# A two-layer encoder step: branch B's decay rows loaded once and kept, its running sums made earlier, and two steps of VectorE placed elsewhere

## The reference, cut to what matters

```python
for l in range(DEPTH):                                   # DEPTH = 2
    p = split_proj(rmsnorm(x, g_norm[l]) @ w_in[l])
    qa, ka, va, qi, ki, wi = a_inputs(p, pos)
    o_a = dsa_prompt(qa, qi, wi, ka, va, ki)             # attends to the top 256 keys by index score
    qb, kb, vb, lf = b_inputs(p, b_f[l])
    o_b = fox_prompt(qb, kb, vb, jnp.cumsum(lf, axis=1)) # branch B, below
    qc, kc, vc = c_inputs(p)
    o_c = band_prompt(qc, kc, vc, c_bias[l])             # own chunk and 8 before it
    mk, mv = mem_kv(mem_prompt, g_mem[l], w_mem_kv[l])
    o_m = mem_attend(m_query(p), mk, mv)                 # 256 memory tokens
    x = x + merge(p, o_a, o_b, o_c, o_m, w_out[l])

def fox_attend(q, k, v, fq, fk, qpos, kpos):
    logits = jnp.einsum('bqhd,bkhd->bhqk', q, k) * HEAD_DIM ** -0.5
    logits = logits + jnp.swapaxes(fq, 1, 2)[..., :, None] - jnp.swapaxes(fk, 1, 2)[..., None, :]
    logits = jnp.where((kpos[None, :] <= qpos[:, None])[None, None], logits, -jnp.inf)
    return jnp.einsum('bhqk,bkhd->bqhd', jax.nn.softmax(logits, axis=-1), v)
```

## Time and profile before

| | |
|---|---|
| median of 3 runs | 1775.59 us (1773.81 to 1777.07) |
| the profiled execution | 1776.22 us |
| its span in the trace | 1774.4 us |
| busy, share of the span | PE 97%, DVE 57%, ACT 39%, POOL 13% |
| mean granted clock of PE | 0.994 |
| DMA | 177.75 MB, 100 GB/s over the span |
| branch B's row loads | 24, of 256 to 1024 KB |

### The profile page before, as it was taken

The page is one execution under the profiler, slowest core; times in us unless marked ns, Lnnn a source line. Parts: engine busy times, 40 slices in busy tenths (PEclk is TensorE's granted clock), DMA queues, the critical chain, the costliest instruction groups (busy, mean ns, idle before and its releaser), DMA issues.

```text
span 1774.4 us, 25988 instructions
## 1 busy us (share of the span) xinstructions
PE 1724.7 (97%) x8678; PEld 902.0 (51%) x8678; DVE 1008.3 (57%) x2709; ACT 692.6 (39%) x1657; POOL 222.0 (13%) x398
## 2 busy tenths in 40 slices
PE   7999999999999899999999999989999999999998
PEld 3544555555555455555444345545555544555553
DVE  3646876787778633332235288767877776333322
ACT  3542333433343344453224323333334433445531
POOL 0232211100000000001012332111000000000000
PEclk9999999999999999999999999999999999999999
DMA  6433533323122222112431425433231223220121
GB/s 249 116 138 90 180 133 132 140 77 105 45 111 90 91 67 76 58 53 64 120 121 49 162 79 178 133 140 121 78 108 42 107 93 96 71 97 36 43 73 46
DMA packets 57026, 177.75 MB, mean 100 GB/s; under 512 B 10128, under 2 KB 24304, under 8 KB 53824
## 3 DMA queue, kind: packets, MB, share of 16 engines
q1 hardware_dynamic: 39424, 125.88, 20.9%
q0 software_dynamic: 17472, 50.22, 8.6%
HBM read 149.09 MB, written 30.07 MB: 101 GB/s over the span
## 4 chain that ended last, share of the span: by engine, by line
PE 87%; DVE 6%; DMA 3%; ACT 2%; issue 2%; ACTq 0%; DVEq 0%; POOL 0%; SPq 0%
PE psX L828 58%; PE psT L786 9%; PE psS L944 6%; PE psX L1011 6%; DMA bias<-scratch_fp 2%; PE psS L856 2%; DVE lower L1221 1%; DVE work L1439 1%; PE psX L986 1%; PE psS L786 1%; PE psS L917 1%; PE psX L786 1%; DVE sc L1382 1%; PE psS L910 0%; PE psS L875 0%
## 5 line engine op out<-in xcount | busy, mean ns | idle before, releaser
L828 PE MATMUL psX<-wring,hT 128*128 128x512 f32 (+1 forms) x2592 | 1170.5, 593 | 5.4 <-ACT gate L1109 3.7
L828 PEld LDWEIGHTS psX<-wring,hT 128*128 128x128 f32 x2592 | 468.8, 191 | 480.5 <-issue 478.3
L1221 DVE TENSOR_SCALAR_CACHE_REDUCE lower<-sc,thr 128x640 uint8<-128x640 f32 (+5 forms) x462 | 407.3, 934 | 19.0 <-issue 12.7
L1160 ACT ACTIVATE work<-work,stat 128x256 f32<-128x256 f32 (+7 forms) x288 | 199.9, 694 | 309.5 <-DVEq L1442 306.4
L1169 ACT COPY work<-psT 128x512 f32<-128x512 f32 (+2 forms) x352 | 157.3, 489 | 339.2 <-PE psT L786 337.3
L786 PE MATMUL psT<-con,work 128*128 128x128 f32 x1080 | 158.9, 279 | 8.8 <-ACT kv L1128 8.8
L786 PEld LDWEIGHTS psT<-con,work 128*128 128x128 f32 x1080 | 123.1, 141 | 85.0 <-issue 73.2
L1439 DVE CUSTOM_DVE_ANT_0 work<-psS,bias 128x640 f32<-128x640 f32 (+7 forms) x144 | 103.8, 721 | 102.0 <-PE psT L786 36.5
L1439 DVE CUSTOM_DVE_ANT_0 work<-psS,sc 128x384 f32<-128x384 f32 (+5 forms) x48 | 42.8, 892 | 78.5 <-PE psT L786 74.8
L1487 POOL DMA_DIRECT2D scratch_oscr<-gate x54 | 30.3, 561 | 373.7 <-DVEq L1473 353.9
L944 PE MATMUL psS<-kv,qT 64*128 64x512 f32 (+3 forms) x384 | 69.9, 482 | 0.0
(11 more groups left out here) (195 smaller groups left out, 1537.7 us busy)
## 6 DMA issues: line engine op xcount, KB each, us to landing
wring<-in_w SPq DMA_DIRECT2D x20, 2048.0 KB, 8.4
cache<-in_kB SPq DMA_DIRECT2D x16, 512.0 KB, 8.0
cache<-in_vB SPq DMA_DIRECT2D x16, 512.0 KB, 5.2
cache<-in_kC SPq DMA_DIRECT2D x16, 512.0 KB, 6.5
cache<-in_vC SPq DMA_DIRECT2D x16, 512.0 KB, 4.9
scratch_oscr<-gate POOLq DMA_DIRECT2D x54, 128.0 KB, 2.0
hT<-scratch_oscr SPq DMA_DIRECT2D x18, 384.0 KB, 3.6
bias<-scratch_fp POOLq DMA_DIRECT2D x6, 1024.0 KB, 5.3
```

Source lines behind the costliest of these rows:

```text
L828: mm = pe.matmul(X.ap(use)[:, 0:w], lhs, wv[:, kt, 0:w], start=(kt == 0), stop=(kt == KT - 1))
L1160: nc.scalar.activation(x, x, ACT.Exp, scale=-1.0, bias=stats(p)[:, 0, i:i + 1], accum_out=stats(p)[:, 1, i:i + 1]).then_inc(probs.sem, 1)
L1221: v.tensor_scalar(lower[:, at:at + STRIP_L[t]], sc[:, o], thr[:, n:n + 1], 0.0, ALU.is_lt, ALU.add, accum_out=below[:, n:n + 1])
```

## The change

1. The decay rows of all four heads are loaded once a layer, for all 1024 keys, in four DMAs (`decays("near")` for the first 256 keys, `decays("far")` for the rest), into `bias` and into `xr`, which isn't in use then. For each tile POOL's `close` copies the tile's own 128 columns of a head pair aside, drains, adds the mask in place, signals and drains; `reopen` copies the plain columns back when the logits are done, and drains. The per-pack loads are gone.
2. `wrow` stands ahead of `Q 3` and of the projection `B2 ST_`.
3. A step Z takes over the inverting and scaling on DVE, and stands ahead of T and L in `advance`, so ahead of the unit's selection.
4. `pace` spreads the selection up to unit (M1, 3).

```diff
--- before.py
+++ after.py
@@ -174,6 +174,8 @@
             if is_sample(pack) and pack[2] + 1 < PAIRS:
                 j = pack[2] + 1
                 emit("Q", (pack[0], f"s{j}", j, 1))
+        if prev:
+            emit("Z", prev)
         if prev and not fresh:
             emit("T", prev, 0)
         if pack:
@@ -282,6 +284,7 @@
         emit("Pp", "B1", ST_, 3, 6)
         emit("iw", 0)
         emit("P", "B1", ST_)
+        emit("wrow")
         emit("Q", 3)
         emit("Pp", "B2", ST_, 0, 3)
         emit("is", 2)
@@ -289,7 +292,6 @@
         emit("is", 3)
         emit("TR", "B1", ST_)
         emit("P", "B2", ST_)
-        emit("wrow")
         emit("Q", ("B", "s0", 0, 1))
 
         units = [(c, t) for pair in (("B1", "B2"), ("C1", "C2")) for t in [ST_] + TILES[:NT] for c in pair][2:]
@@ -303,7 +305,7 @@
 
                 rounds += topk_steps()
                 spare[0] = 0.0
-                pace[0] = sum(cost(x) for x in rounds) / (units.index(("A2", ST_)) - units.index(("B1", 0)) - 1)
+                pace[0] = sum(cost(x) for x in rounds) / (units.index(("M1", 3)) - units.index(("B1", 0)) - 1)
             settle()
             if t < NT and c in ("B2", "C2", "M1", "A2"):
                 queue += packs_of(c[0], t)
@@ -513,7 +515,10 @@
         bias = sb("bias", H * 5 * P + SKEYS)
         gateA = bias[:, 0:(NT + 1) * W].rearrange("p (t c) -> p t c", c=W)
         gmem = bias[:, 0:D]
-        rows_b = bias[:, 0:2 * D]
+
+
+        dec = [bias[:, 0:2 * SEQ].rearrange("p (h c) -> p h c", h=2), xr[:, :, :]]
+        plain = bias[:, 2 * SEQ:2 * SEQ + H * P].rearrange("p (g h c) -> p g h c", g=2, h=2)
         strips = bias[:, 0:H * 5 * P].rearrange("p (h c) -> p h c", h=H)
         sbias_ = bias[:, H * 5 * P:]
 
@@ -623,7 +628,7 @@
         cache_loaded = [Signal(sem(f"cache{k}_loaded"), cache_loads[k::RING], lambda u: 16 * cdmas(u)) for k in range(RING)]
 
         b_packs = [p for p in packs if p[1][0] == "B" and not is_sample(p[1])]
-        pbias = Signal(sem("prompt_bias_loaded"), b_packs, lambda e: 16)
+        pbias = {e: Signal(sem(f"decays_{e}_loaded"), each(e), lambda e: 32) for e in ("near", "far")}
         masked = Signal(sem("prompt_bias_masked"), b_packs)
         strips_loaded = Signal(sem("strips_loaded"), each("C"), lambda e: 16)
         sbias_loads = [("B", j) for j in range(PAIRS)] + [("C", 0)]
@@ -675,11 +680,6 @@
             if br == "A":
                 return hT[:, first:first + n, t * P:(t + 1) * P]
             return gate[:, t, first * P:(first + n) * P].rearrange("p (g c) -> p g c", g=n)
-
-        def decays(pack):
-
-            n, L = heads(pack), blocks(pack) * P
-            return rows_b[:, 0:n * L].rearrange("p (h c) -> p h c", h=n)
 
         def tile_of(l, n):
 
@@ -1416,7 +1416,7 @@
                             b_ = sbias_[:, 0:L]
                         elif br == "B":
                             dve.wait_ge(*masked.on(p))
-                            b_ = decays(p)[:, i, :]
+                            b_ = dec[h // 2][:, h % 2, 0:L]
                         elif br == "C":
                             if (h, t) == (0, 0):
 
@@ -1440,7 +1440,7 @@
                         if i >= heads(p) - 2:
                             last.then_inc(S.empty(u).sem, 1)
                         dve.drain().then_inc(logits.sem, 1)
-                elif k == "T" and s[2] == buffers(s[1])[-1]:
+                elif k == "Z":
 
                     p = s[1]
                     br, t, h0, nh = p
@@ -1504,19 +1504,33 @@
                         pool.dma_start(d["xr"][h * P:(h + 1) * P, :], d["xl"][h:h + 1, :].to_broadcast([P, XL])
                                        ).then_inc(lines.sem, 16)
 
-            def prompt_bias(p):
+            def decays(part):
+
+                c0, c1 = {"near": (0, 2 * P), "far": (2 * P, SEQ)}[part]
+                for g_ in range(2):
+                    src = bass.AP(d["fp"].tensor, 2 * g_ * SEQ + c0, [[0, P], [SEQ, 2], [1, c1 - c0]])
+                    pool.dma_start(dec[g_][:, :, c0:c1], src).then_inc(pbias[part].sem, 16)
+
+            def close(p):
 
                 _, t, h0, n = p
-                L = (t + 1) * P
-                src = bass.AP(d["fp"].tensor, h0 * SEQ, [[0, P], [SEQ, n], [1, L]])
-                pool.dma_start(decays(p), src).then_inc(pbias.sem, 16)
-
-            def prompt_mask(p):
-
-                own = decays(p)[:, :, blocks(p) * P - P:]
-                pool.wait_ge(*pbias.on(p))
-                g.tensor_tensor(own, own, con[:, C_TRI:C_TRI + P].unsqueeze(1).to_broadcast([P, heads(p), P]), ALU.add
-                                ).then_inc(masked.sem, 1)
+                part = "near" if t < 2 else "far"
+                pool.wait_ge(*pbias[part].on(part))
+                tri = con[:, C_TRI:C_TRI + P].unsqueeze(1).to_broadcast([P, 2, P])
+                for g_ in range(h0 // 2, (h0 + n) // 2):
+                    g.tensor_copy(plain[:, g_], dec[g_][:, :, t * P:(t + 1) * P])
+                pool.drain()
+                for g_ in range(h0 // 2, (h0 + n) // 2):
+                    last = g.tensor_tensor(dec[g_][:, :, t * P:(t + 1) * P], plain[:, g_], tri, ALU.add)
+                last.then_inc(masked.sem, 1)
+                pool.drain()
+
+            def reopen(p):
+
+                _, t, h0, n = p
+                for g_ in range(h0 // 2, (h0 + n) // 2):
+                    g.tensor_copy(dec[g_][:, :, t * P:(t + 1) * P], plain[:, g_])
+                pool.drain()
 
             def own_halves(q, j, hp, heads_, gg=0):
 
@@ -1605,9 +1619,10 @@
                     store(d["fp"], work[0:4, 3, :], f_dma.sem)
                     store(d["fs"], work[0:32, 2, P:P + SKEYS], f_dma.sem)
                     pool.wait_ge(*f_dma.on("out"))
-                    prompt_bias(packs_of("B", 0)[0])
+                    decays("near")
                     sample_bias("B", 0)
-                    prompt_mask(packs_of("B", 0)[0])
+                    decays("far")
+                    close(packs_of("B", 0)[0])
                 elif k == "Q" and s[1] in range(PAIRS):
 
                     j = s[1]
@@ -1647,11 +1662,12 @@
                         sample_bias(*sbias_loads[h0 + 1])
                     elif br == "B":
                         pool.wait_ge(*logits.on(last_logits))
-                        i = b_packs.index((l, p))
-                        if p != last_pack["B"]:
-                            prompt_bias(b_packs[i + 1][1])
-                            prompt_mask(b_packs[i + 1][1])
-                        else:
+                        if t + 1 < NT:
+                            reopen(p)
+                            for later in packs_of("B", t + 1):
+                                if later[2] >= p[2] and later[2] + later[3] <= p[2] + p[3]:
+                                    close(later)
+                        elif p == last_pack["B"]:
 
                             src = bass.AP(d["xr"].tensor, P - 1, [[XL - 1, P], [P * XL, H], [1, 5 * P]])
                             pool.dma_start(strips, src).then_inc(strips_loaded.sem, 16)
```

## The result

The changed kernel takes 1804.71 us (median of 4 runs, 1798.86 to 1806.94) against 1776.2 us (4 runs); the ratio is 1.0158, with a 95% interval of 1.013 to 1.0185. It is slower by some 28 us, where the forecast said 211. Its profiled execution took 1798.86 us and was the fastest of the four, so sums against its trace are sums to 1798.86.

A forecast was written before the change was run, and what follows sets the result against it. PE was taken to bound the kernel, with POOL's drains the bound in branch B. From 1776.2 us: +216.2 for both layers, -8.3 inverted sums, +4.5 masks, forecast 1987 us (chance 0.64); own range 1940 to 2045, stretched to 1780 to 2045.

The forecast's parts named there:

- The bound: Whole kernel: TensorE (PE) busy for 97% of the span, so an edit pays only by closing a PE gap.
- The sign: Whole kernel: slower than before, with chance 0.88; within the error 0.08, faster 0.04.
- the term that decides: POOL's `close` and `reopen`: 34 new drains a layer, 68 in all, taken at 6.7 us each.
- the 216 us of the walk: Branch B: POOL, slowed by its drains, becomes the bound; each layer grows by 108.1 us, +216.2 in both.
- The early sums without drains: Before `is 3`: PE waits for `Q 3` behind `wrow`, 10.4 us a layer, bounds 8.2 to 14.7.
- Rival 2: Only the first drain of each `wrow`, after a long pause, costs 6.7 us more: 1796 us, chance 0.12.
- The gains: PE gaps closed: 14.0 us by decay rows kept on chip, 10.3 us by inverted sums ahead of selection.
- the kv waits: PE's two waits for ACT's kv copy, 8.8 us, one in each layer; claimed to go with decay rows kept.
- The selection's pace: Last unit of C2 and first of M1: masks delay ACT's copies, +4.5 us in all, bounds -4 to +12.

## Why the prediction was right and wrong

**The bound** was read rightly: PE sets the time, and each edit's effect was found as a gap of PE. The sign was right too, and so was the place of the loss: `Q 3` behind `wrow`, `is 3` behind `Q 3`.

**The step that failed is the term that decides: 6.7 us for each of 68 drains.** Three long drains were all the trace of before had, all of them after many DMAs of POOL or with some in flight. I excluded DMAs in flight as the cause because the last of them had none, and so kept one fixed price for all. The reading missed that there can be two causes, either of which makes a drain long: DMAs in flight, and what POOL has done since the last drain. In branch B a drain meets no DMA in flight and at most five issued since the one before, and took 0.45 to 1.5 us. With that POOL isn't the bound there, and the 216 us of the walk are gone. What I should have asked of the three rows is what POOL had done since its last drain, not which instruction stood just ahead.

**The early sums without drains** were priced at 10.4 us a layer. The kernel with semaphores showed 12.3 and 12.0, the early sums alone 10.3 and 9.3. This term held. With drains I had 23.8; the trace shows 17.7 and 19.8: one long drain, and a second of 1.5 us that lies mostly beside the additions.

**Rival 2** gave 1796 us and came within 9 us of the median, 3 of the profiled execution. The range of 1780 to 2045 holds the measured median only because it was stretched to this rival; the forecast's own range began at 1940. Its description of what happens (the first drain of each `wrow` dear, the rest cheap) was right, its reason (the long pause) was not: the added drain showed it. So its number is good for a reason that it didn't have.

**The gains** were summed at 24.3 us; at the old pace and without the stall they were 25. The sum was right and the split was wrong. I booked the kv waits to the kept rows, as if only the absence of a load could remove a wait for a load. Z alone brought them from 8.8 to 0.8 us (and left one row stall of 3.0 us elsewhere), and beside Z and the early sums the kept rows' own share is within the error.

**The selection's pace** was priced at 4.5 us with bounds of -4 and +12, and measures 8.5 with Z in place. The mechanism (masks in the first M1 units, ACT's copies behind them) was right, and the term was under-sized in the waits: I had 5 to 6 us a layer against 3.5, the traces of the two kernels show 6.5 against 3.1. The clock, which I had counted in, added nothing between them. Alone, without Z, it costs 19 us, outside the bounds; the prediction had priced it with Z there, and didn't say that it leant on that.

**The sum by measured terms**: 1776.2 - 25 (gains) + 8.5 (pace) + 37.5 (waits for qs) + 3.2 (clock behind them) = 1800 us, against 1798.86 profiled.

## What to carry to other kernels

Before moving a step up, list who stands behind it in each in-order queue that it enters: here one swap of two lines turned a loss of 1.6% into a gain of 1.0%. A drain on a queue that issues DMAs waits for those DMAs, so where one operation must only see another's result, a semaphore on that operation is the cheaper fence. And a stall of the bottleneck belongs to no single edit: try each part alone before booking it.

## What the hardware showed that I had not expected

- A drain of GpSimd took 0.45 to 1.5 us with none of its DMAs in flight and up to five issued since the one before, 4.4 to 10.6 with some in flight, and 3.09, 7.09 and 8.71 us with none in flight but 32, 118 and 109 issued since (77, 196 and 244 rows of GpSimd in the trace).
- GpSimd waiting on a semaphore of its own copy started the next operation 0.08 us after it.
- A row load of 896 KB took 9.9 or 6.5 us beside the same 2048 KB weight load, which was issued 0.52 or 0.69 us after it; one of 1024 KB took 11.0 us with the weight load issued at the same moment.
- PE waits of 2.1 to 2.2 us were followed by 3.4 us at a granted clock of 0.50 in three of four cases in the kernel after, and two such waits of the kernel with `Q 3` ahead by none. Behind waits of 17.7 and 19.8 us the stretch was 3.2 and 3.3 us, behind waits of 16.3 and 5.5 us it was 5.4 and 6.1: in these runs the loss didn't grow with the length of the wait.
